# Folding the norm's per-channel weight into the projection weights, and moving the preparation of the next token tiles within a block

## What is computed

```python
def rms_norm(x, g):
    y = x * lax.rsqrt(jnp.mean(x * x, axis=-1, keepdims=True) + EPS)
    return y * g                      # g = ln_g, one number per channel (1024)

xn   = rms_norm(h, ln_g)
proj = xn @ w_in                      # 1024 x 4112, columns split:
# qkv_a 1536 | a 8 | b 8 | z_a 512 | q_b 512 | k_b 512 | v_b 512 | z_b 512
```

## Time and profile before

| | us |
|---|---|
| median of 3 runs | 3692.42 |
| lowest, highest | 3684.9, 3701.24 |
| the profiled execution | 3691.9 |
| its span, first to last instruction | 3690.1 |
| TensorE busy in it | 3383.2 (92%) |
| VectorE, ScalarE, GpSimd busy | 2200.3, 1356.4, 1042.6 |

### The profile page before, as it was taken

The page is one execution under the profiler, slowest core; times in us unless marked ns, Lnnn a source line. Parts: engine busy times, 40 slices in busy tenths (PEclk is TensorE's granted clock), DMA queues, the critical chain, the costliest instruction groups (busy, mean ns, idle before and its releaser), DMA issues. The chain is left out here.

```text
span 3690.1 us, 68597 instructions
## 1 busy us (share of the span) xinstructions
PE 3383.2 (92%) x26375; PEld 2886.7 (78%) x26375; DVE 2200.3 (60%) x4410; ACT 1356.4 (37%) x2617; POOL 1042.6 (28%) x1314
## 2 busy tenths in 40 slices
PE   6999999969998999997877577999997999999998
PEld 5899899958876888886777455888885888888887
DVE  6777687746987968771566455666674232323332
ACT  4445454433223323211556324666663111111111
POOL 4333233328996635400566400000000000000000
PEclk9999999979999999998999787999998999999999
DMA  5444344444337452434765543222224121212121
GB/s 173 130 132 138 119 140 131 119 145 152 124 99 214 145 164 93 131 103 137 238 224 196 135 138 109 87 73 87 73 70 170 60 68 61 68 61 68 61 68 36
DMA packets 325228, 437.33 MB, mean 119 GB/s; under 512 B 190452, under 2 KB 213268, under 8 KB 320327
## 3 DMA queue, kind: packets, MB, share of 16 engines
q1 hardware_dynamic: 324942, 433.47, 38.0%
HBM read 276.56 MB, written 159.46 MB: 118 GB/s over the span
## 5 line engine op out<-in xcount | busy, mean ns | idle before, releaser
L88 PE MATMUL b_psP<-b_w_hi,b_xT_hi 128*128 128x512 f32 x1320 | 519.6, 394 | 38.6 <-DVE b_xT_lo L1331 21.5
L89 PE MATMUL b_psP<-b_w_lo,b_xT_hi 128*128 128x512 f32 x1320 | 517.6, 392 | 0.0
L90 PE MATMUL b_psP<-b_w_hi,b_xT_lo 128*128 128x512 f32 x1320 | 517.2, 392 | 0.0
L88 PE MATMUL a_psG<-a_xT_hi,a_w_hi 128*128 128x256 f32 (+1 forms) x1536 | 456.6, 297 | 38.3 <-DVE a_xT_lo L680 31.4
L89 PE MATMUL a_psG<-a_xT_lo,a_w_hi 128*128 128x256 f32 (+1 forms) x1536 | 443.8, 289 | 0.0
L90 PE MATMUL a_psG<-a_xT_hi,a_w_lo 128*128 128x256 f32 (+1 forms) x1536 | 443.3, 289 | 0.0
L88 PEld LDWEIGHTS a_psG<-a_xT_hi,a_w_hi 128*128 128x128 f32 x1536 | 298.6, 194 | 60.2 <-DVE a_xT_lo L680 35.2
L88 PEld LDWEIGHTS b_psP<-b_w_hi,b_xT_hi 128*128 128x128 f32 x1320 | 250.3, 190 | 96.9 <-DVE b_xT_lo L1331 44.9
L697 DVE SCALAR_TENSOR_TENSOR a_act<-a_raw,a_taps,a_act 128x256 f32<-128x256 f32 x576 | 306.1, 531 | 20.6
L89 PEld LDWEIGHTS a_psG<-a_xT_lo,a_w_hi 128*128 128x128 f32 x1536 | 298.3, 194 | 0.0
L90 PEld LDWEIGHTS a_psG<-a_xT_hi,a_w_lo 128*128 128x128 f32 x1536 | 298.1, 194 | 0.0
(11 more groups left out here) (368 smaller groups left out, 7203.2 us busy)
## 6 DMA issues: line engine op xcount, KB each, us to landing
rows_b<-b_rows SPq DMA_DIRECT2D x165, 256.0 KB, 2.2
b_x_full<-xT SPq DMA_DIRECT2D x78, 512.0 KB, 4.3
qkvB<-a_act SPq DMA_DIRECT2D x16, 1536.0 KB, 5.3
d_conv_T<-qkvB SPq DMA_DIRECT2D x16, 1536.0 KB, 10.1
xT<-a_x_full SPq DMA_DIRECT2D x33, 512.0 KB, 5.8
h_mixed<-mixed SPq DMA_DIRECT2D x33, 512.0 KB, 4.1
out<-h_y SPq DMA_DIRECT2D x33, 512.0 KB, 2.9
a_x<-in_x_prompt SPq DMA_DIRECT2D x32, 512.0 KB, 4.5
```

Of the source, the lines that this page charges most:

```text
L88: nc.tensor.matmul(out, x_hi, w_hi, start=first, stop=False)
L89: nc.tensor.matmul(out, x_hi, w_lo, start=False, stop=False)
L90: return nc.tensor.matmul(out, x_lo, w_hi, start=False, stop=last)
```

## The change

`ln_g` no longer multiplies the token tiles. `channel_gain` and its semaphore are gone from GpSimd, and `full` waits for the tile's load instead. The weights are scaled: in `project_a`, an even piece is scaled in ScalarE's rounding activation and VectorE's low part becomes one scalar_tensor_tensor; an odd piece is first scaled in place by an extra activation, and GpSimd subtracts as before. The 32 columns of the gates are scaled once on GpSimd. In `project_b`, the factor is loaded again (one small DMA behind the first tile's load), ScalarE's activation takes it as its scale and VectorE's subtraction becomes a scalar_tensor_tensor.

The preparation moves. With two tiles ahead it is now: square 0 and 3, norm 0 and 3, spread 2 and 6, full 2 and 6, split_hi 3 and 7, split_lo 3 and 7 (in block 0 the second square and norm stay at 5). A third tile: square and norm 6, spread and full 9, both splits 10. SyncE's order in `project_a` is untouched. The diff, cut to its core:

```diff
@@ lo_part
-            eng.tensor_tensor(w_lo[:, k, a:b], stage[m % SLOTS][:, 0:b - a], w_hi[:, k, a:b].bitcast(F32),
-                              ALU.subtract).then_inc(done, 1)
+            if m % 2:
+                eng.tensor_tensor(w_lo[:, k, a:b], stage[m % SLOTS][:, 0:b - a], w_hi[:, k, a:b].bitcast(F32),
+                                  ALU.subtract).then_inc(done, 1)
+            else:
+                eng.scalar_tensor_tensor(w_lo[:, k, a:b], stage[m % SLOTS][:, 0:b - a], lnT[:, k:k + 1], w_hi[:, k, a:b].bitcast(F32),
+                                         ALU.mult, ALU.subtract).then_inc(done, 1)
@@ GpSimd
-            channel_gain(0)
             norm(0)
...
+            pool.wait_ge(w_ab_in, 16)
+            pool.tensor_tensor(w_ab[:, :, :], w_ab[:, :, :], lnT[:, :].unsqueeze(2).to_broadcast([P, KT, PCOLS]), ALU.mult)\
+                .then_inc(ab_scaled, 1)
...
                     if g == 0 and ahead:
                         norm(ahead[0])
-                        channel_gain(ahead[0])
-                    if g == 5 and len(ahead) > 1:
+                    if g == (3 if b else 5) and len(ahead) > 1:
                         norm(ahead[1])
-                        channel_gain(ahead[1])
-                    if g == 8 and len(ahead) > 2:
+                    if g == 6 and len(ahead) > 2:
                         norm(ahead[2])
-                        channel_gain(ahead[2])
@@ ScalarE
-                e.activation(w_hi[:, k, a:b], stage[m % SLOTS][:, 0:b - a], ACT.Copy).then_inc(w_hi_ok, 1)
+                x = stage[m % SLOTS][:, 0:b - a]
+                if m % 2:
+                    e.activation(x, x, ACT.Copy, scale=lnT[:, k:k + 1]).then_inc(w_scaled, 1)
+                    e.wait_ge(w_scaled, m // 2 + 1)
+                    e.activation(w_hi[:, k, a:b], x, ACT.Copy).then_inc(w_hi_ok, 1)
+                else:
+                    e.activation(w_hi[:, k, a:b], x, ACT.Copy, scale=lnT[:, k:k + 1]).then_inc(w_hi_ok, 1)
...
                         if g == 0:
                             square(ahead[0])
-                        if g == 4:
+                        if g == 3:
                             split_hi(ahead[0])
                     if len(ahead) > 1:
-                        if g == 5:
+                        if g == (3 if b else 5):
                             square(ahead[1])
-                        if g == 9:
+                        if g == 7:
                             split_hi(ahead[1])
@@ TensorE
-                    if g == 3 and ahead:
+                    if g == 2 and ahead:
                         spread(ahead[0])
-                    if g == 8 and len(ahead) > 1:
+                    if g == 6 and len(ahead) > 1:
                         spread(ahead[1])
@@ VectorE
-                v.wait_ge(gained, t + 1)
+                v.wait_ge(xT_in[t % XBUFS], 16 * (t // XBUFS + 1))
...
-                    if g == 8 and len(ahead) > 1:
+                    if g == 6 and len(ahead) > 1:
                         full(ahead[1])
-                    if g == 9 and len(ahead) > 1:
+                    if g == 7 and len(ahead) > 1:
                         split_lo(ahead[1])
@@ project_b
+                sp.dma_start(lnT[:, :], d.ln_g.rearrange("(k p) -> p k", p=P)).then_inc(ln_in, 16)
...
-                e.activation(w_hi[SLOT[seg]][:, k, :], there, ACT.Copy).then_inc(w_hi_ok, 1)
+                e.activation(w_hi[SLOT[seg]][:, k, :], there, ACT.Copy, scale=lnT[:, k:k + 1]).then_inc(w_hi_ok, 1)
...
-                v.tensor_tensor(w_lo[SLOT[seg]][:, k, :], staged(seg, k)[0], w_hi[SLOT[seg]][:, k, :].bitcast(F32),
-                                ALU.subtract).then_inc(w_lo_ok, 1)
+                v.scalar_tensor_tensor(w_lo[SLOT[seg]][:, k, :], staged(seg, k)[0], lnT[:, k:k + 1],
+                                       w_hi[SLOT[seg]][:, k, :].bitcast(F32), ALU.mult, ALU.subtract).then_inc(w_lo_ok, 1)
```

More of the change, by code:

```diff
@@ L192, in project_a @@
         xT_in = [ph.sem(f"a_xT_in{i}") for i in range(XBUFS)]
-        gained = ph.sem("a_gained")
+        ab_scaled = ph.sem("a_ab_scaled")
+        w_scaled = ph.sem("a_w_scaled")
         rstd_ps = ph.sem("a_rstd_ps")
@@ L409, in norm @@
                 pool.tensor_tensor(rstd[:, a:a + 1], var[:, a:a + 1], neg_half[:, a:a + 1], ALU.pow).then_inc(rstd_ok, 1)
-            def channel_gain(t):
-                x = x_full[t % XBUFS]
-                pool.wait_ge(xT_in[t % XBUFS], 16 * (t // XBUFS + 1))
-                pool.tensor_tensor(x[:, :, :], x[:, :, :], lnT[:, :].unsqueeze(2).to_broadcast([P, KT, P]), ALU.mult)\
-                    .then_inc(gained, 1)
             def halos(b, g):
@@ L442, in _ @@
                 if i == 2:
-                    channel_gain(1)
                     norm(1)
+            pool.wait_ge(w_ab_in, 16)
+            pool.tensor_tensor(w_ab[:, :, :], w_ab[:, :, :], lnT[:, :].unsqueeze(2).to_broadcast([P, KT, PCOLS]), ALU.mult)\
+                .then_inc(ab_scaled, 1)
             for b in range(BLOCKS):
@@ L500, in _ @@
             square(0)
+            e.wait_ge(ln_in, 16)
             hi_part(0)
@@ L547, in _ @@
                             square(ahead[0])
-                        if g == 4:
+                        if g == 3:
                             split_hi(ahead[0])
                     if len(ahead) > 1:
-                        if g == 5:
+                        if g == (3 if b else 5):
                             square(ahead[1])
-                        if g == 9:
+                        if g == 7:
                             split_hi(ahead[1])
                     if len(ahead) > 2:
-                        if g == 7:
+                        if g == 6:
                             square(ahead[2])
-                        if g == 11:
+                        if g == 10:
                             split_hi(ahead[2])
@@ L593, in gate_product @@
                 if t == 0:
-                    pe.wait_ge(w_ab_in, 16)
+                    pe.wait_ge(ab_scaled, 1)
                 if q:
@@ L646, in _ @@
                         query_sums(b - 1)
-                    if g == 3 and ahead:
+                    if g == 2 and ahead:
                         spread(ahead[0])
-                    if g == 8 and len(ahead) > 1:
+                    if g == 6 and len(ahead) > 1:
                         spread(ahead[1])
-                    if g == 10 and len(ahead) > 2:
+                    if g == 9 and len(ahead) > 2:
                         spread(ahead[2])
@@ L738, in gates @@
                     v.reciprocal(beta[:, :], bden[:, :]).then_inc(ab_v, 1)
+            v.wait_ge(ln_in, 16)
             for i in range(HALVES // 2):
@@ L759, in _ @@
                         lo_part(v, HALVES + 2 * g, w_lo_v)
+                    if g == 2 and ahead:
+                        full(ahead[0])
                     if g == 3 and ahead:
-                        full(ahead[0])
-                    if g == 4 and ahead:
                         split_lo(ahead[0])
-                    if g == 8 and len(ahead) > 1:
+                    if g == 6 and len(ahead) > 1:
                         full(ahead[1])
-                    if g == 9 and len(ahead) > 1:
+                    if g == 7 and len(ahead) > 1:
                         split_lo(ahead[1])
+                    if g == 9 and len(ahead) > 2:
+                        full(ahead[2])
                     if g == 10 and len(ahead) > 2:
-                        full(ahead[2])
-                    if g == 11 and len(ahead) > 2:
                         split_lo(ahead[2])
@@ L947, in project_b @@
         norm_g = ph.sb("b_norm_g", [P, 2, DB])
+        lnT = ph.sb("b_lnT", [P, KT])
         ones = ph.sb("b_ones", [P, C])
@@ L965, in project_b @@
         consts = ph.sem("b_consts")
+        ln_in = ph.sem("b_ln_in")
         filled = ph.sem("b_filled")
@@ L1133, in _ @@
             load_x(0)
+            with nc.allow_non_contiguous_dma(reason="small per-channel constants, once"):
+                sp.dma_start(lnT[:, :], d.ln_g.rearrange("(k p) -> p k", p=P)).then_inc(ln_in, 16)
             for k in range(KT):
```

## The result

The changed kernel takes 3706.42 us (median of 19 runs, 3694.39 to 3716.3), the kernel before 3698.1 us in 19 runs beside them (3681.24 to 3705.7). The ratio is **1.0027, 95% interval 1.0015 to 1.0038**: slower by a little, less than the 0.5% that I had set as no change, but above my 3691, just outside my range (3706 at its upper end), and on the side of a loss. Of the 15.4 us between 3691 and 3706.42, 5.7 are the reference: I had counted from 3692.42, the median of three runs, and the kernel before stands at 3698.1 in the 19. The change itself I put at -1.3, and it is +8.3.

The account below looks back on a forecast made before the run. The prediction took TensorE, at 92% of the span, as the bound. Its terms, -1.7 + 2.2 + 0 - 2.5 + 0.7 = -1.3 us, gave 3691 us from a median of 3692.42, range 3667 to 3706.

Parts of the forecast that it names:

- (1): Blocks 1 to 6 and 10 to 14: 11 periods of 43.5 us for 43.66, -1.7 us, ends -6 and +5.
- (2): Block 7, with a third tile: TensorE waits 9.1 us for 6.89 at block 8, +2.2, ends 0 and +4.
- (3): Blocks 8 and 9: block 8 hides ScalarE's wait, block 9 has none at its end; 0, ends -1 and +1.
- (4): Block 0: low-part weight waits of 6.8 us go, extra activations come; -2.5 us, ends -5 and +1.
- (5): Start of `project_b`: one more small load delays the weight loads; +0.7 us, ends 0.4 and 2.
- the moved square waits for its load: ScalarE's square, moved earlier, waits until T + 5.8 for a load issued behind all four kq stores; about 60 us in all.
- the loop that follows: Through ScalarE's wait, VectorE and the kq copies: period 44.1 us against 41.85 of TensorE's own work.
- T: The end of a block's fourth kq copy on ScalarE, from which the loop's steps are counted in us.
- the open term: What GpSimd's query squares cost VectorE: 0.7 or 1.7 us, a loop of 43.1 or 44.1; 43.5 taken.
- Rival A: VectorE makes up ScalarE's wait and TensorE's own work sets the period; about -22 us, 3670 us; chance 0.21.
- Rival B: Third kq copy waits for the first's store, period 46.1 us; +28 us, 3720 us; chance 0.13.
- Rival C: The load, not its place in the order, sets everything: no effect beyond block 0, -2 us; chance 0.66 with the forecast.

Follow-up runs that it names:

- e10: e6 with GpSimd's query squares of a block moved into the next block, ahead of the halo of its group 4; ratio 1.0016 to the kernel before.
- e6: The changed kernel with both gate products of a block put behind its group 11; ratio 1.0080 to the kernel before.
- e4: The changed kernel with only the second tile's square and norm put back at group 5; ratio 0.9950 to the kernel before.
- e3: The changed kernel with the load of the second tile ahead issued before the second key-query store, not behind all four; ratio 0.9922 to the kernel before.
- e1: The changed kernel with the weight scaling kept and all steps of the tiles ahead put back at their old groups; 3671.63 us, ratio 0.9930 to the kernel before.
- e2: The kernel before, gain products kept, with only the steps of the tiles ahead moved to their new groups; 3730.6 us, ratio 1.0094 to the kernel before.
- e5: e3 with the second tile's spread, full and split in block 0 back behind groups 8 and 9; 3667.29 us, ratio 0.9923 to the kernel before.
- e8: The changed kernel with the load of the second tile ahead issued before the fourth key-query store; ratio 0.9932 to the kernel before.
- e9: e3 with the steps of both tiles ahead in block 0 back at their old groups; 3662.77 us, ratio 0.9913 to the kernel before.
- e7: e1 with two unused 128x512 GpSimd products in each gain's place, in blocks 0 to 7 only; ratio 0.9960 to the kernel before.
- e12: The changed kernel with the steps of both tiles ahead in block 0 back at their old groups; ratio 1.0025 to the kernel before.
- e11: e2 with the load of the second tile ahead issued before the second key-query store; ratio 0.9997 to the kernel before.

## Why the prediction was wrong

By its own terms, measured in the two traces between the last kq copies of the blocks (us):

| term | predicted | measured |
|---|---|---|
| (1) blocks 1 to 6 and 10 to 14 | -1.7 | +8.3 |
| (2) block 7 | +2.2 | +2.8 |
| (3) blocks 8 and 9 | 0 | +1.7 |
| (4) block 0 and the start | -2.5 | +3.4 |
| (5) start of `project_b` | +0.7 | +0.6 |
| all behind it | 0 | -5.4 |
| sum | -1.3 | +11.5 |

Term (1) is off by 10.0 and term (4) by 5.9; these two make the miss of the change.

- **Right: the moved square waits for its load, and the loop that follows.** I had T + 1.3 for the issue (1.3), T + 5.8 for the square (6.2), T + 9.35 for VectorE (9.7), T + 34.2 for the end of the first kq copy (34.3: 312.54 - 278.25) and a loop of 44.1 (44.4). The sum of ScalarE's waits was 77 us for the 60 I named.
- **Wrong, the step that failed: the open term.** Between 43.1 and 44.1 I took the middle, 43.5, because the query squares would overlap the low split. They did not: 2.00 for 0.41 in the trace. Their price in these rows is 1.6, close to the 1.7 of the earlier trace rows; in e10 the period of the block read fell by 1.4, those at full clock by 1.2 in the mean. The bound that I had worked out and set aside, 44.1, was the right one, and the rule of the Trainium skill that I had cited gave it. Seven periods of after at full clock are 43.94 to 44.65, 44.31 in the mean: 11 x (44.31 - 43.66) = +7.2 of the +8.3. In term (1) the granted clock is below full in three before and in four after (43.90, 46.90, 46.17, 45.29); that is the rest.
- **Wrong: where TensorE waits.** I named 1 to 2 us on `a_kq` in 10 blocks. That list stayed at 10.3 us in 5. I had followed ScalarE's wait to VectorE, but not through each wait of TensorE on ScalarE: `take_rows` stands on ScalarE behind the copy of group 8, and the gate product behind group 9 needs it by T + 18. The entry was in the list before, 1.2 us. It cost the mechanism, not the size, because my loop is as long (e6). It also shows in term (3): block 9, which I had put at nothing, has this wait too (1.51), and its period is 45.18 for 43.63.
- **Wrong: block 0, and its bound.** The waits on `a_w_lo`, 6.8, did go. But I left the square and norm of block 0 at group 5 and never asked whether the spread, moved to 6, would find them: 9.47 of wait. My upper end was +1, and the table has +3.4; e4, with the same block 0, stands 1.1 under the kernel before at that copy, so how much of the +3.4 is this wait stays open.
- **Right: `project_b`. Right by luck: block 7.** I had +2.2 from a wait of 9.1 at block 8 for 6.89. That wait is 4.70, shorter than before. The term came out at +2.8 because of 3.09 at the gate product of that block, and a granted clock of 0.92 for 0.94 over the period.
- **Rival A** had the wait on the load made up by VectorE. That did not happen. e3, which takes the wait away, shows what A promised: periods of 41.78 for A's 42.15, and 27 us under the kernel before in runs beside it, for 22. **Rival B** did not decide: ScalarE's kq copies wait for the store in 12 places, 21.2 us (3 places, 10.5 us before), but in most of the periods only 0.7, and every period above 45.2 has a clock below full. **Rival C** is refuted by e1 and e2.
- **What I valued wrongly at the start**: the gain was worth 1.5 per period, and I saw it, but as one line in a loop that the moves had made longer. As a change of its own it gives 42.1 for 43.66, 25 us in all.

## What to carry to other kernels

When a step is moved ahead in an engine's order, ask for each of its operands where that load is issued, and issue it earlier in the same edit; one load moved in SyncE's queue turned a loss of 0.3% into a gain of 0.8%. Follow a delay through every wait that another engine has on the delayed one, small entries of the wait list too, and not only through the longest chain. When two edits come together, price each alone: here one was worth 25 us, and the other hid it.

## What the runs showed of the hardware

- TensorE's granted clock, by block periods (2 to 6 and 9 to 14, eleven in all, one execution of each kernel): full, the level of 2.4 GHz, in all eleven in e1, e3, e4, e5, e8 and e9. It is 0.96 over the period in two before (45.27 and 45.17 us for 43.66), in three after, in two of the five with the product in e7, in six in e10, in two in e12 and in one in e11; in e6 seven and in e2 eight are below full, down to 0.93. In the two of the kernel before TensorE is busy 1.5 us longer with the same 396 products (43.35 for 41.86); the waits are the same 1.8 us in the periods that fell and in those beside them. So a short wait in each block goes with a fall now and then, but does not tell in which block. In e1 the waits at block starts and on `a_w_lo` fell by 19.7 us, and `project_b` starts 23.6 us earlier: that gain is larger than the waits that it removes.
- A 128x384 activation with a scale per partition takes 602 ns where the plain one took 513, and in `project_b`, at 128x512, 715 for 624; the fused subtraction on VectorE takes 1089 for 934. I had taken both as free. The length of `project_b`, given above with and without them, leaves about 1 us in the mean for them, less than the scatter. The Trainium skill, page ScalarE: Activation LUTs, section What ACT_TABLE_LOAD costs, gives about 93 ns more for each per-partition operand of an activation; the trace agrees with 89 and 91.
